# Gate sessions of a hybrid decoder kernel: four k blocks for each session in place of two

## What is computed

```python
def _layer(x, c, pos, state, lb, g_norm, w_ada, b_ada, w_in, conv_w, conv_b,
           b_i, b_f, skip, w_gn, w_out):
    mod = jax.nn.silu(c) @ w_ada + b_ada            # w_ada: 2048 x 6144
    shift, scale, gate = jnp.split(mod, 3, axis=-1)
    h = _rmsnorm(x, g_norm) * (1.0 + scale[:, None, :]) + shift[:, None, :]
    cols = jnp.split(h @ w_in, np.cumsum(COL_SIZES)[:-1].tolist(), axis=-1)
    ...
    q_r = _rope(_to_heads(rq, H_RT), pos)
    k_r = _rope(_to_heads(rk, H_RT), pos) * HEAD_DIM ** -0.5
    ...
    y = x + gate[:, None, :] * (o @ w_out)
```

## Time and profile before

| what | value |
|---|---|
| three runs, median (lowest to highest) | 2364.67 us (2363.71 to 2365.46) |
| the profiled execution | 2364.68 us |
| its span on the core | 2361.9 us |
| TensorE matmuls busy | 2307.8 us, 98% |
| VectorE busy | 1295.5 us, 55% |
| GpSimd busy | 933.4 us, 40% |
| ScalarE busy | 754.4 us, 32% |
| DMA moved | 347.22 MB, mean 147 GB/s |

### The profile page before, as it was taken

How to read it: one execution, slowest core, us unless ns; L and a number is a source line. 1 busy time by engine, 2 the same in 40 slices (tenths; PEclk the granted TensorE clock), 3 DMA queues, 4 the chain that set the end, 5 groups by cost and what they waited for, 6 DMA issues and landing times.

```text
span 2361.9 us, 50425 instructions
## 1 busy us (share of the span) xinstructions
PE 2307.8 (98%) x21251; PEld 2174.6 (92%) x21251; DVE 1295.5 (55%) x2527; ACT 754.4 (32%) x1219; POOL 933.4 (40%) x668
## 2 busy tenths in 40 slices
PE   5899999999999999999999999999999999999998
PEld 3799999999999999998888999999999999999998
DVE  4465666677776333442227566566777744345444
ACT  2243332333333333321114333233333333334111
POOL 1143443433334334463333343333333443346552
PEclk8999999999999999999999999999999999999999
DMA  9972334544544444368787233354454444433343
GB/s 365 357 223 74 91 92 110 130 135 137 140 136 125 136 137 123 110 190 264 242 284 220 74 91 92 92 141 132 133 139 130 124 124 127 121 97 109 108 118 107
DMA packets 473483, 347.22 MB, mean 147 GB/s; under 512 B 18702, under 2 KB 417514, under 8 KB 471938
## 3 DMA queue, kind: packets, MB, share of 16 engines
q1 hardware_dynamic: 473258, 344.02, 49.9%
HBM read 312.07 MB, written 32.09 MB: 146 GB/s over the span
## 4 chain that ended last, share of the span: by engine, by line
PE 83%; DVE 6%; DMA 4%; ACT 2%; DVEq 2%; SPq 1%; issue 1%; POOL 1%; ACTq 0%; POOLq 0%
PE pj L727 66%; PE mx L733 3%; DVE t L1601 2%; PE mx L1092 2%; PE mx L1118 2%; DMA spare_piece<-in_w_ada 1%; DVE dt L1595 1%; PE mx L848 1%; PE mx L1106 1%; PE mx L814 1%; PE pj L1223 1%; PE mx L1070 1%; ACT t L1305 1%; PE mx L1120 1%; PE mx L1110 1%
## 5 line engine op out<-in xcount | busy, mean ns | idle before, releaser
L727 PE MATMUL pj<-hh,whi 128*128 128x260 f32 x4928 | 1421.1, 288 | 3.4 <-DVE hl L1601 3.1
L695 POOL TENSOR_TENSOR wlo<-raw,whi 128x512 fp32r<-128x512 f32 x632 | 887.8, 1435 | 1343.1 <-ACT whi L1305 1343.1
L727 PE MATMUL pj<-hl,whi 128*128 128x260 f32 x4928 | 1391.8, 282 | 0.0
L727 PE MATMUL pj<-hh,wlo 128*128 128x260 f32 x4928 | 1391.3, 282 | 0.0
L727 PEld LDWEIGHTS pj<-hh,whi 128*128 128x128 f32 x4928 | 928.3, 188 | 54.1 <-issue 48.9
L727 PEld LDWEIGHTS pj<-hl,whi 128*128 128x128 f32 x4928 | 928.8, 188 | 0.0
L727 PEld LDWEIGHTS pj<-hh,wlo 128*128 128x128 f32 x4928 | 927.6, 188 | 0.0
L1305 ACT ACTIVATE whi<-raw 128x2048 fp32r<-128x2048 f32 x158 | 302.8, 1917 | 252.0 <-PE pj L727 183.5
L1305 ACT ACTIVATE xv<-pj 128x260 f32<-128x260 f32 x188 | 64.8, 383 | 397.6 <-PE pj L727 397.3
L1601 DVE SCALAR_TENSOR_TENSOR o<-pj,mod,t 128x260 f32<-128x260 f32 (+1 forms) x56 | 24.6, 480 | 230.2 <-PE pj L727 214.6
L1305 ACT ACTIVATE t<-t 128x520 f32<-128x520 f32 (+1 forms) x125 | 78.9, 631 | 173.0 <-DVEq L1855 126.4
(11 more groups left out here) (308 smaller groups left out, 2318.1 us busy)
## 6 DMA issues: line engine op xcount, KB each, us to landing
raw<-in_w_in SPq DMA_DIRECT2D x256, 512.0 KB, 5.3
raw<-in_w_out SPq DMA_DIRECT2D x64, 512.0 KB, 5.6
lev<-in_w_ada SPq DMA_DIRECT2D x39, 512.0 KB, 5.8
rows<-in_w_ada SPq DMA_DIRECT2D x16, 1024.0 KB, 12.4
out<-ss SPq DMA_DIRECT2D x32, 512.0 KB
lev<-in_w_ada SPq DMA_DIRECT2D x62, 256.0 KB, 4.3
gate_b<-in_w_ada SPq DMA_DIRECT2D x57, 256.0 KB, 4.8
xv<-in_w_ada SPq DMA_DIRECT2D x25, 512.0 KB, 5.9
```

The costliest lines, as they stand in the source:

```text
L695: last = e.tensor_tensor((wlo_third if t == 2 else wlo[:, par, :])[:, cs], w[:, cs], high_of(t)[:, cs].bitcast(F32), ALU.subtract)
L727: last = e.matmul(pj[:, 2 * par + b, 0:HALF], w[:, par, kb * P:(kb + 1) * P], x[:, kb, b * HALF:(b + 1) * HALF], start=(kb == 0 and m == 0 ...
```

## The change

Four pieces are summed in one session: there are 16 sessions in layer 0 and 12 in layer 1, with 32 matmul instructions each. In layer 0 they fill heads 5 to 9 and x = 0 of head 10, in layer 1 heads 5 to 8. The two further buffers are columns 0 to 511 and 512 to 1023 of `rope_t`, so the second load of the rope table moves from head 5 to head 10, behind a wait for the layer's last session. The sessions of a head stand behind part 5 of tile 1, part 2 of tile 2 and part 7 of tile 2.

```diff
-SESSIONS = (32, 24)
+SESSIONS = (16, 12)
+SESSION_K = 4
...
-        gate_a = levf[:, LEVELS * T - 512:LEVELS * T]
+        gate_at = (levf[:, LEVELS * T - 512:LEVELS * T], gate_b, rope_t[:, 0:512], rope_t[:, 512:1024])
...
-        gate_in = [sem(f"gate_in{j}") for j in range(2)]
+        gate_in = [sem(f"gate_in{j}") for j in range(SESSION_K)]
...
-                        block, k = divmod(session + 8 * l, 8)
-                        for j, at in enumerate((gate_a, gate_b)):
+                        block, k = divmod(session + 4 * l, 4)
+                        for j, at in enumerate(gate_at):
                             e.dma_start(at, w_ada[l].rearrange("(k p) n -> p k n", p=P)
-                                        [:, 2 * k + j, 2 * D + 512 * block:2 * D + 512 * (block + 1)]).then_inc(gate_in[j], 16)
+                                        [:, SESSION_K * k + j, 2 * D + 512 * block:2 * D + 512 * (block + 1)]).then_inc(gate_in[j], 16)
...
-                    if h == FIRST_ML:
-                        e.wait_ge(head_done, l * NH + FIRST_ML + 1)
+                    if h == FIRST_ML + H_ML - 1:
+                        e.wait_ge(gate_used, l * SESSIONS[0] + SESSIONS[l])
                         e.dma_start(rope_t, rope_d).then_inc(rope_in, 16)
...
-                    for i, at in enumerate((gate_a, gate_b)):
+                    for i, at in enumerate(gate_at):
                         e.wait_ge(gate_in[i], 16 * (l * SESSIONS[0] + session + 1))
                         for j in range(4):
-                            last = e.matmul(mx[32 * j:32 * j + 32, 3, x * P:(x + 1) * P], sct[:, 2 * (session % 8) + i, :],
-                                            at[:, j * P:(j + 1) * P], start=(i == 0), stop=(i == 1))
+                            last = e.matmul(mx[32 * j:32 * j + 32, 3, x * P:(x + 1) * P], sct[:, SESSION_K * (session % 4) + i, :],
+                                            at[:, j * P:(j + 1) * P], start=(i == 0), stop=(i == SESSION_K - 1))
                     last.then_inc(gate_used, 1)
...
-                        for j, part, x in ((0, 7, 0), (1, 3, 1), (1, 7, 2)):
+                        for j, part, x in ((0, 5, 0), (1, 2, 1), (1, 7, 2)):
                             own[j][part] = own[j].get(part, ()) + (lambda x=x: gate_session(h, x),)
...
-                            block, src = session // 8 + l, mx[:, 3, x * P:(x + 1) * P]
-                            if session % 8:
+                            block, src = session // 4 + l, mx[:, 3, x * P:(x + 1) * P]
+                            if session % 4:
```

## The result

The changed kernel takes 2386.91 us (median of five runs, 2381.53 to 2387.66) where the kernel before takes 2364.30 (median of five runs). The ratio is 1.0087 with a 95% interval of 1.0077 to 1.0098: slower. The forecast was slower, 2374 us, with a range up to 2382; the time lies 4.9 us above that range. The profiled execution took 2387.66 us, its span is 2385.9.

The account below looks back on a forecast made before the run. TensorE's own issue time and the waits before it were taken to bound the kernel. From 2364.68 us, -5.6 - 1.3 + 16.3 = +9.4 gave 2374 us, range 2357 to 2382.

Parts of the forecast that it names:

- Term 1: TensorE's switches between projection and small session matmuls: 28 sessions fewer at 0.20 us each, -5.6 us.
- Term 2: TensorE's wait before ml_conv in mLSTM heads: filled in eight heads, -2.8 us, longer in two, +1.5; together -1.3 us.
- Term 3: VectorE: 28 sums fewer, 10 us of its time, costed at nothing because VectorE stood idle before them.
- Term 4: Session x = 1: last piece lands 2.5 us later, stalling TensorE in seven heads, +16.3 us; bounds 5 and 21 us.
- Rival C: TensorE's clock falls behind the stalls, 48 matmuls at 1.2 GHz, seven times 6 us added: 2416 us; chance 0.03.
- Rival A: At session x = 1 the pieces come in time and the kernel is faster: 2358 us; chance 0.2.
- Rival D: Session x = 2 stalls too, up to 1 us in nine heads: 2383 us; no separate chance given.

Follow-up runs that it names:

- experiment 7: Changed kernel with session x = 0 behind part 3 of tile 1 and the load of session x = 1 issued ahead of the fetch: 2354.56 us, ratio 0.9961.
- 8: Kernel before (two pieces, 56 sessions) with the same order and places as experiment 7: 2363.56 us, ratio 0.9997.
- experiment 9: The changed kernel run and profiled once more, with nothing altered: 2380.25 us, ratio 1.0073.
- experiment 6: Changed kernel with the load of session x = 1 issued ahead of the weights' load, directly behind the fetch: 2358.71 us, ratio 0.9975.
- experiment 1: Changed kernel with 12 extra 128x128 matmuls (24 instructions), results never read, in front of session x = 1 in heads 6 to 10: 2379.06 us, ratio 1.0062.

## Why the prediction was wrong in size

- **Term 1, -5.6 us: mis-sized, it is -9.2.** It let 16 further small matmuls cost 0.57 us and each switch 0.20. In experiment 7 a session of 32 stands so:

```profile
481.22 0.28 PE L728 MATMUL pj<-hl,whi 128*128 128x260 f32 x1
481.43 0.43 PE L815 MATMUL mx<-lev,sct 128*32 128x128 f32 x8
481.68 0.40 PE L815 MATMUL mx<-gate_b,sct 128*32 128x128 f32 x8
481.89 0.62 PE L815 MATMUL mx<-lev,sct 128*32 128x128 f32 x16
482.44 0.39 PE L728 MATMUL pj<-hh,whi 128*128 128x260 f32 x1
482.67 0.29 PE L728 MATMUL pj<-hh,wlo 128*128 128x260 f32 x1
```

  From 481.22 to 482.67 are 1.45 us where a session of 16 has 1.01. So 16 further instructions cost 0.44 us, the other 0.33 of a session's 0.77 goes with each session that is saved, and 28 x 0.33 = 9.2 us. The heads agree: an mLSTM head with three doubled sessions is 57.95 us for 57.00, +0.95, and 3 x 0.44 - 0.35 is +0.97, where the prediction's terms give +1.36. A retention head without its three sessions is 55.3 us before and 52.9 after, 2.36 us for a forecast 2.3.
- **Term 2, -1.3 us: right.** The wait before ml_conv is gone in eight heads, and in heads 9 and 10 of layer 1 it is longer, as forecast (1.25 us from start to start in both, for 0.47). Terms 1 and 2 together would give some -10.5; the spans give -9.3 (experiment 7 against before) and -8.7 (7 against 8). Where the last microsecond stays was not found.
- **Term 3, nothing: right.** 28 VectorE instructions and 21 us of its busy time are gone, and the span does not show it.
- **Term 4, the mechanism and the seven heads: right; the size was not.** Hold-ups of 24.7 us in the first profile and 18.7 in the second stand for the 16.3 of the sum. Two parts were off. First, "the last piece lands 2.5 us later": it was 3.5 and 2.7, of which the two pieces are 1.8 (a rate gave 1.6) and the slip of the weights behind the fetch is 1.7 and 0.9 (forecast 0.9). Second, when it is needed: since small matmuls cost less than term 1 had it, the last piece is wanted 9.3 us from the table's mark and not 9.6, over seven heads 2.3 us more of waiting. With these, 7 x (12.9 - 9.3) = 25 and 7 x (12.0 - 9.3) = 19 us, as measured. The upper bound, 21, lies between the two. The order of the heads was right in the first profile: longest in head 6 of layer 1 (5.2), shortest in head 9 (2.2); in the second head 7 of layer 1 is the longest.
- **Rival C was the step that failed**, at a chance of 0.03 and with nothing in the sum. The clock did fall, behind five of the seven sessions, and cost 8.6 us (6.1 in experiment 9, behind four). Without it the profiled execution would have been near 2379 us, inside the range. "A TensorE wait of 1 us in a stretch of 6 us did not lower it" was true and proved nothing for the waits of up to 4.0 us that the prediction itself had worked out. Nor was the trace of before silent on longer ones. In its first 80 us TensorE waits 5.1 us from start to start for a DMA, and the granted clock behind is 0.50 (timeline of TensorE, and the view by windows):

```profile
73.19 0.44 PE L794 MATMUL mx<-xv,sct 128*32 128x128 f32 x4 [4.83 <-DMA xv<-in_w_ada]
```

```profile
69.70:76.40 6.70, 3.21 (x38) 2.70 (x39) 5.89 (x12) 4.55 (x6) 0.50 (x1) 0.50 1.05 386
```

  The price of C was wrong the other way: not 6 us a place but 1.5 to 1.7. C let 48 matmuls behind each wait run at 1.2 GHz; the stretches were 3.4 or 6.8 us long, and part of each lay in the hold-up itself.
- **The errors partly cancel.** Hold-ups and clock were put too low, the gain of term 1 too. That experiment 9 gives 2380.25 us, inside the range, does not save the forecast: 6.1 us of it are the clock's, which the sum had at nothing.
- **Rival A** would have needed a place in the queue that this change did not give it; experiment 7 shows it is real there. Rival D, waits at x = 2, did not come: in the changed kernel no session x = 2 was held up.
- **The fit of the page "DMA: Bandwidth & Descriptors"**, section "Anatomy of one DMA — SWDGE (gpsimd) path" of the Trainium skill, is for DMAs of another issuing engine; an estimate by it has weights and four pieces in after 6.8 us. They took from 475.14 to 485.4, 10.2 us. The measurement decides, against the estimate both before and after.
- **The range** ended at 2382. With the clock's cost it should have gone to some 2390: 2364.7 - 6.9 + 21 + 7 = 2386, and more since the hold-ups reached 24.7. Rival D's own sum, 2383, was already outside it.

Open: what sets the time in which the stores in front of the fetch land. It differs between executions of one kernel: in head 8 of layer 0 the fetch slipped by 2.4 us in the first profile and by 1.1 in the second, and in head 6 of layer 1 it slipped by 1.9 us in the first and came 0.8 us earlier than before in the second. Open as well: what exactly lowers the clock (see the last section).

## What to carry to other kernels

Doubling what one step loads moves everything behind its issues in the same queue; ask for each what the queue waits for next, and put the load that is wanted soonest into a gap in which the queue only waits for something else. A gain of fewer switches is real, but it is small (0.3 us a session here), and one late transfer of 3 us takes back ten of them. Where a forecast wait is longer than the ones looked at, look through the whole trace for one as long, its first microseconds too, and price the clock. And profile a kernel that waits for transfers more than once before its waits are explained to a tenth of a microsecond.

## What was not expected of the hardware

In the changed kernel's first profile the clock fell to 0.50 behind waits that from the last projection matmul to the first session matmul were 2.26 us and longer, five times, and not behind those of 1.39 and 1.97 us. The length alone does not decide it. In experiment 6 it fell behind a session that was held up by some 2 us between its pieces, with no wait in front, and here it stayed at 1.00 behind a hold-up of 2.8 us in all (head 8 of layer 1). Between the layers a TensorE wait of 2.4 us left it at 1.00 in the kernel before, and in experiment 1 it fell behind the same wait. 24 small matmuls in the wait kept it at 1.00 in experiment 1.

Two extra pieces, 0.43 us of issuing each, moved a fetch 15 us later in the queue by 0.8 to 1.5 us.

Sixteen further small matmuls in a session that is already running cost 0.44 us, while sixteen in a session of their own cost 0.77.
